# Where modulation rows, a feed-forward split and a rounding stand in a three-layer kernel

## Chip, cores and metric

One core of one Trainium2 chip runs the whole program in one launch. The metric is the device time of one execution in microseconds (us). TensorE is called PE, VectorE DVE, ScalarE ACT, GpSimd POOL; SyncE (SP) only issues transfers. DMA is the set of 16 engines that move data between device memory and on-chip memory.

## The reference, cut to what matters

The input is 256 tokens of 1024 float32 features. Three layers follow one another:

```python
h = x                                        # first_block, two layers
h = h + rg_lru_block(rms_norm(h, mix_norm[0]))            # layer 0
h = h + swiglu_ffn(rms_norm(h, ffn_norm[0]))
h = h + stick_breaking_attention(rms_norm(h, mix_norm[1]))  # layer 1
h = h + swiglu_ffn(rms_norm(h, ffn_norm[1]))
x = rms_norm(h, final_norm)
...
mod = silu(c) @ w_ada + b_ada                # second_block: 6 * 1024 modulation values
sh1, sc1, g1, sh2, sc2, g2 = split(mod, 6)
x = x + g1 * (mixed_attentions(rmsnorm(x) * (1 + sc1) + sh1) @ w_out)
x = x + g2 * moe(rmsnorm(x) * (1 + sc2) + sh2)            # 32 experts, top 2 of one group
return rmsnorm(x, final_g)
```

In `rg_lru_block` the input product has a recurrent branch (convolution, two sigmoid gates from products with `gate_w`, a scan) and a gate branch (a gelu); their product goes through `w_out`. `swiglu_ffn` has 2816 hidden columns. `c` is a single row of 1024, so `mod` is a product of one row with a 1024 x 6144 matrix (25 MB) that nothing needs before the third layer.

## The kernel before

The program is written by hand, one instruction list per engine, with semaphores. Activations lie feature-major: 8 tiles of 128 features by 256 tokens. Weights come in units of 2 MB into a ring of three places (`RING`), or, for the feed-forwards, in steps of 256 hidden columns into two slots. SP issues all of these loads in one order and waits for the place to be free.

**Products in parts.** Most float32 products are made as three matmuls of a coarser type. A weight is split first: ACT rounds it into a high part (`hi_unit`, `split_g`, `split_u` on ACT), DVE subtracts to get the low part (`lo_unit`, `split_g`, `split_u` and `subtract` on DVE, line 1057), and PE multiplies high by high, low by high, high by low (lines 1645, 1670, 1735). So PE follows DVE, which follows ACT, which follows a load.

**A feed-forward** has 11 steps. In each PE makes gate and up products (`gate_up`, line 1735, 96 matmuls) and the down product of the step before (`down`, line 1670, 48 matmuls). DVE does in each step: `split_g` of the next step, the product of silu and up, its two parts, `split_u` of the next step, the split of the down weight, and in layer 0 then some units of the modulation.

**Modulation rows.** The 48 columns of `mod` are 24 units of two. POOL loads a unit (1 MB, line 599) into one of two places in the ring when the unit two before is used up; DVE multiplies each of its two columns with the row silu(c) and sums (`ada_product`, line 1135). `ADA_FROM` says which units step n of the first feed-forward does at its end: 2, 2, 3, 2, 3, 2, 3, 2, 2, 1 units in steps 0 to 9, unit 22 at the end of step 10 and unit 23 in its middle. The ring place is free for `k0` (a weight of the attention) when all 24 are used. The row silu(c) is made on ACT (line 807) just before the norm of the first feed-forward; `silu_c` tells DVE.

**A norm** goes ACT squares (line 655), PE sums over features (line 1615), ACT root (lines 659, 660), DVE scales (line 1032). It cannot start until DVE has added the residual (line 1189 after the LRU, line 1198 after the feed-forward). DVE and PE have little to do meanwhile: a pause.

**The gates** of the LRU: after convolution of half the features (line 1103 ends it) PE makes four gate tiles, then four more for the other half (line 1691). The tiles go round four banks, so the fifth waits until ACT has taken the first with its sigmoid (line 728). In ACT's list the rounding of `gb0` (first half of the gate branch weight) stands ahead of all sigmoids and that of `gb1` behind the fourth.

**The experts.** After routing, each of 32 experts needs 6 MB. SP loads three ahead into three slots and issues the next expert's weights when PE has used a slot. Before the first of these (expert 3) SP issues two small transfers, `gate_tile` (line 566): the row g2 spread over 128 partitions, which DVE needs ahead of its work for expert 0 (lines 1550 to 1558).

**At the start** PE runs 24 small matmuls on ones (line 1677), then the sums of the first norm, then the product with `rec0` (line 1636).

## Time and profile before

| what | value |
|---|---|
| median of 3 runs | 1341.46 us (1340.09 to 1345.76) |
| the profiled execution | 1343.59 us |
| its span, first to last instruction | 1341.8 us |
| mean granted clock of PE | 0.943 of full |
| PE matmul busy | 1154.9 us (86%) |
| DVE busy | 634.5 us (47%) |
| ACT busy | 412.1 us (31%) |
| DMA, mean over the span | 270 GB/s |
| modulation rows | DVE line 1135, 56.1 us busy in 48 products |

PE is busy through the first two thirds of the span, where it moves little data; from about 905 us on DMA is busy in every slice at about 429 GB/s and PE waits for expert weights. A microsecond saved ahead of that stage moves the whole stage.

### The profile page before, as it was taken

To read this page: it belongs to the slowest core of one execution; us is meant where nothing else is said; L and a number is where in the kernel's file an instruction comes from. 1 tells how busy PE (TensorE), PEld (TensorE's weight loads), DVE (VectorE), ACT (ScalarE), POOL (GpSimd) and SP (SyncE) were. 2 spreads that over 40 slices of the span, in tenths; PEclk is the share of its full clock that TensorE was granted. 3 is DMA by queue.
4 is the path that set the end of the run, shared out by engine and by line. 5 is a ranking of instruction groups with operands and counts; after the bars stand their busy time and mean duration, and the time that the engine had idled before them with its cause. 6 is when DMAs were issued, how large, how long until landed. Compare 5 with 4: busy or idle time off the path is not lost.

```text
span 1341.8 us, 22971 instructions
## 1 busy us (share of the span) xinstructions
PE 1154.9 (86%) x9327; PEld 933.6 (70%) x9329; DVE 634.5 (47%) x997; ACT 412.1 (31%) x519; POOL 31.6 (2%) x69
## 2 busy tenths in 40 slices
PE   9998999999989899999899999967876568567666
PEld 8898999998977899999799888842332223223223
DVE  5686777765435254455634887471211112111213
ACT  3854333333357243334514565250000000000001
POOL 0000000000000000000000000000000000000000
PEclk9999999999999999999899999978988889888889
DMA  9565988872550575552644433499999999999996
GB/s 350 205 256 179 334 288 326 287 268 91 186 188 1 203 260 177 178 177 72 121 139 170 144 127 134 179 370 422 429 429 427 430 428 428 429 427 429 429 427 262
DMA packets 99464, 362.47 MB, mean 270 GB/s; under 512 B 4160, under 2 KB 51664, under 8 KB 84176
## 3 DMA queue, kind: packets, MB, share of 16 engines
q1 hardware_dynamic: 95376, 335.32, 65.5%
q0 software_dynamic: 3888, 26.24, 4.9%
q8 instruction: 43, 0.70, 0.2%
q14 instruction: 13, 0.11, 0.0%
q10 hardware_dynamic: 144, 0.10, 0.0%
HBM read 360.58 MB, written 1.06 MB: 270 GB/s over the span
## 4 chain that ended last, share of the span: by engine, by line
PE 64%; DMA 24%; DVE 5%; ACT 4%; issue 2%; SPq 0%; POOLq 0%; POOL 0%; DVEq 0%; ACTq 0%
DMA wbuf<-in_w_up 21%; PE ps L1735 17%; PE ps L1670 13%; PE ps L1645 8%; PE ps L2030 6%; PE ps L1908 4%; PE ps L1636 3%; PE ps L1654 3%; DMA wbuf<-in_w_ada 2%; PE ps L1615 2%; DVE parts L1057 2%; PE ps L2050 1%; PE ps L2080 1%; DVE wbuf L1135 1%; DMA wbuf<-in_lru_w_in 1%
## 5 line engine op out<-in xcount | busy, mean ns | idle before, releaser
L1735 PE MATMUL ps<-big_parts,parts 128*128 128x256 f32 x2112 | 266.4, 289 | 12.2 <-DVE parts L1057 6.7
L1735 PEld LDWEIGHTS ps<-big_parts,parts 128*128 128x128 f32 x2112 | 262.7, 197 | 14.9 <-DVE parts L1057 7.3
L1057 DVE TENSOR_TENSOR parts<-wbuf,parts 128x2048 fp32r<-128x2048 f32 x88 | 200.0, 2290 | 132.0 <-ACT parts L797 43.4
L2030 PE MATMUL ps<-wbuf,big 128*32 128x256 f32 x2176 | 166.7, 472 | 108.7 <-DMA wbuf<-in_w_up 97.8
L2030 PEld LDWEIGHTS ps<-wbuf,big 128*32 128x32 f32 x2176 | 86.1, 134 | 203.0 <-issue 101.4
L1670 PE MATMUL ps<-big_parts,parts 128*128 128x256 f32 x1344 | 166.1, 283 | 1.1 <-DVE parts_f L1259 1.1
L1670 PEld LDWEIGHTS ps<-big_parts,parts 128*128 128x128 f32 x1344 | 163.3, 192 | 1.3 <-issue 1.3
L989 ACT ACTIVATE big<-ps 128x128 f32<-128x128 f32 x33 | 9.1, 277 | 417.3 <-PE ps L2030 417.3
L1562 DVE TENSOR_TENSOR big<-big,ps 128x128 f32<-128x128 f32 x33 | 9.5, 289 | 265.1 <-ACT big L989 265.1
L1645 PE MATMUL ps<-parts_f,parts 128*128 128x256 f32 x672 | 97.3, 284 | 0.0
L1645 PEld LDWEIGHTS ps<-parts_f,parts 128*128 128x128 f32 x672 | 87.9, 192 | 0.2
L2080 PE MATMUL ps<-wbuf,big 128*32 128x512 f32 x544 | 65.4, 596 | 16.2 <-DVE big L1550 16.2
L1057 DVE TENSOR_TENSOR parts<-wbuf,parts_f 128x2048 fp32r<-128x2048 f32 x28 | 63.3, 2289 | 23.5 <-ACT parts_f L688 23.5
L2050 PE MATMUL ps<-big 64*128 64x512 f32 x272 | 68.3, 615 | 3.6 <-DVE big L1558 2.6
L707 ACT ACTIVATE parts<-wbuf 128x2048 fp32r<-128x2048 f32 x22 | 42.1, 1915 | 87.5 <-PE ps L1735 80.7
L1135 DVE SCALAR_TENSOR_TENSOR wbuf<-wbuf,big 128x1024 f32<-128x1024 f32 x48 | 56.1, 1221 | 20.0 <-DMA wbuf<-in_w_ada 20.0
L797 ACT ACTIVATE parts<-wbuf 128x2048 fp32r<-128x2048 f32 x20 | 38.3, 1913 | 60.6 <-PE ps L1670 60.6
L688 ACT ACTIVATE parts_f<-wbuf 128x2048 fp32r<-128x2048 f32 x28 | 52.4, 1904 | 3.3 <-PE ps L1645 3.3
L1908 PE MATMUL ps<-parts_f 128*128 128x256 f32 x256 | 48.5, 291 | 1.0 <-DVE parts L1057 1.0
L2050 PEld LDWEIGHTS ps<-big 64*128 64x128 f32 x272 | 23.6, 186 | 35.6 <-issue 33.9
L688 ACT ACTIVATE parts<-wbuf 128x2048 fp32r<-128x2048 f32 x22 | 40.9, 1908 | 23.4 <-DMA wbuf<-in_lru_w_in 22.8
L1636 PE MATMUL ps<-big,wbuf 128*128 128x256 f32 x192 | 43.9, 391 | 3.8 <-ACT big L665 2.2
(312 smaller groups left out, 1332.4 us busy)
## 6 DMA issues: line engine op xcount, KB each, us to landing
wbuf<-in_w_down SPq DMA_DIRECT2D x32, 2048.0 KB, 37.9
wbuf<-in_w_gate SPq DMA_DIRECT2D x31, 2048.0 KB, 32.6
wbuf<-in_w_up SPq DMA_DIRECT2D x31, 2048.0 KB, 37.1
wbuf<-in_ffn_w_in SPq DMA_DIRECT2D x44, 1024.0 KB, 11.4
wbuf<-in_w_ada POOLq DMA_DIRECT2D x24, 1024.0 KB, 8.3
wbuf<-in_ffn_w_out SPq DMA_DIRECT2D x22, 1024.0 KB, 5.0
wbuf<-in_w_in SPq DMA_DIRECT2D x10, 2048.0 KB, 8.0
wbuf<-in_attn_w_qkv SPq DMA_DIRECT2D x6, 2048.0 KB, 7.9
```

The source lines that it names most:

```text
L688: nc.scalar.activation(halves(unit_parts(name)[0])[i], halves(unit_view(name))[i], ACT.Copy).then_inc(w_hi, 1)
L707: nc.scalar.activation(fg_part[0], ffn_views(slot)[0], ACT.Copy).then_inc(fg_hi, 1)
L1057: nc.vector.tensor_tensor(lo, whole, hi.bitcast(F32), ALU.subtract).then_inc(done, 1)
L1135: ins = nc.vector.scalar_tensor_tensor(out=w, in0=w, scalar=1.0, in1=c_row, op0=ALU.mult, op1=ALU.mult, accum_out=ada[:, at:at + 1])
L1636: ins = mm(b[:, d * 256:(d + 1) * 256], w[:, k, (m + d) * P:(m + d + 1) * P], rhs[:, k], start=(k == 0), stop=(k == kn - 1))
L1645: ins = mm(b[:, d * 256:(d + 1) * 256], w[pw][:, k, (m + d) * P:(m + d + 1) * P], rhs[px][:, k], start=(k == 0 and i == 0), stop=(k == kn ...
L1670: ins = mm(ps[:, 4 + f // 2, (f % 2) * 256:(f % 2 + 1) * 256], w[:, k, f * P:(f + 1) * P], r, start=(first and k == 0 and f % 2 == 0), sto ...
L1735: ins = mm(ps[:, b, d * 256:(d + 1) * 256], w[pw][:, k, d * P:(d + 1) * P], h_part_of[px][:, k], start=(k == 0 and i == 0), stop=(k == KC ...
L1908: ins = mm(ps[:, c % 2, d * 256:(d + 1) * 256], w[pw][:, k, m * P:(m + 1) * P], x_part[px][:, k], start=(k == 0 and i == 0), stop=(k == KC ...
L2030: ins = mm(at, rows, gu_place[s][:, :, k, r * P:(r + 1) * P], start=(k == 0), stop=(k == KC - 1))
L2050: ins = mm(ps[:, 4 + 2 * c + h, :], comb[q][rows, c * P:(c + 1) * P], yE[q][rows, :], start=False, stop=stop, skip_group_check=True)
L2080: ins = mm(ps[r * WIN:(r + 1) * WIN, 2, :], hidT[:, f * WIN:(f + 1) * WIN], d_place[s][:, f, h * 512:(h + 1) * 512], start=(i == 0), stop= ...
```

## The change

The modulation units are laid out anew: unit 0 is done before the residual that follows the LRU, step n of the first feed-forward does units 2n + 1 and 2n + 2, step 10 does unit 21 in its middle and unit 22 at its end, and unit 23 comes after that feed-forward's residual. For unit 0, ACT makes silu(c) earlier, between its `split_g` and `split_u`. DVE's `split_u` of the first step moves behind the residual. ACT rounds `gb0` after the two sigmoids of gate tile 0 and `gb1` after those of tile 1. The warm-up has 20 matmuls in place of 24. The two transfers of `gate_tile` go from SP's list to POOL's; SP waits for the first gate and up product (`first_gu`) in their place.

```diff
-WARM_UP = 24
+WARM_UP = 20
-ADA_FROM = (0, 2, 4, 7, 9, 12, 14, 17, 19, 21, 22)
+ADA_FROM = tuple(range(1, ADA_UNITS - 1, 2))
@@ SP
-            sp.wait_ge(mod_stored, 48)
-            sp.wait_ge(spread_pe, 2)
-            for h in range(2):
-                sp.dma_start(gate_tile[h * HALF_ROWS:(h + 1) * HALF_ROWS], mod_dram[2:3, h * 512:(h + 1) * 512].to_broadcast([HALF_ROWS, 512])).then_inc(gate_in, 16)
+            sp.wait_ge(first_gu, 1)
@@ POOL, after the slot numbers and before its wait for info_ready
+            pool.wait_ge(mod_stored, 48)
+            pool.wait_ge(spread_pe, 2)
+            for h in range(2):
+                pool.dma_start(gate_tile[h * HALF_ROWS:(h + 1) * HALF_ROWS], mod_dram[2:3, h * 512:(h + 1) * 512].to_broadcast([HALF_ROWS, 512])).then_inc(gate_in, 16)
@@ ACT
             hi_unit("rec1")
-            hi_unit("gb0")
             for n in range(4):
...
-                if n == 1:
-                    hi_unit("gb1")
+                if n < 2:
+                    hi_unit(f"gb{n}")
...
             split_g(0, ffn_loads(0, 0))
+            act.wait_ge(c_in, 16)
+            nc.scalar.activation(c_row, c_row, ACT.Silu).then_inc(silu_c, 1)
             wait_used(act, "lo0")
             split_u(0)
...
-            act.wait_ge(c_in, 16)
-            nc.scalar.activation(c_row, c_row, ACT.Silu).then_inc(silu_c, 1)
@@ DVE
             split_g(0, 0)
-            split_u(0, 0)
...
             dve.wait_ge(silu_c, 1)
+            ada_unit(0)
             wait_used(dve, "lo1")
             for k in range(KC):
...
+            split_u(0, 0)
@@ DVE, a step of the feed-forward
-                            ada_unit(ADA_UNITS - 1)
+                            ada_unit(ADA_UNITS - 3)
...
-                        for u in range(ADA_FROM[n], ADA_FROM[n + 1] if following else ADA_UNITS - 1):
+                        for u in range(ADA_FROM[n], ADA_FROM[n + 1]) if following else (ADA_UNITS - 2,):
                             ada_unit(u)
@@ DVE
             add_residual(f"ffn0_{FFN_STEPS - 1}")
+            ada_unit(ADA_UNITS - 1)
```

## Rows read from the trace of the kernel before

**Rows 1.** The page's chain of work that ended last: shares of the span by engine.

```profile
PE 64%; DMA 24%; DVE 5%; ACT 4%; issue 2%; SPq 0%; POOLq 0%; POOL 0%; DVEq 0%; ACTq 0%
```

**Rows 2.** Timeline, an undisturbed step: start, duration, engine, line, operation, [idle <- releaser].

```profile
283.61 5.92 PE L1670 MATMUL ps<-big_parts,parts 128*128 128x256 f32 x48
...
289.37 11.68 PE L1735 MATMUL ps<-big_parts,parts 128*128 128x256 f32 x96
```

**Rows 3.** Timeline, the first stall in the first feed-forward.

```profile
163.48 0.53 POOL L599 DMA_DIRECT2D wbuf<-in_w_ada  x1 [14.46 <-DVE wbuf L1135]
...
172.01 1.23 DVE L1135 SCALAR_TENSOR_TENSOR wbuf<-wbuf,big 128x1024 f32<-128x1024 f32 x1 [6.54 <-DMA wbuf<-in_w_ada]
...
176.65 13.26 PE L1735 MATMUL ps<-big_parts,parts 128*128 128x256 f32 x96 [2.76 <-DVE parts L1057]
```

**Rows 4.** Busy time by stretch: length, PE, PEld, DVE, ACT, POOL, clock, DMA share, GB/s.

```profile
133.40:156.50 23.10, 23.10 (x195) 23.10 (x194) 19.43 (x21) 8.64 (x6) 1.59 (x3) 1.00 1.01 374
156.50:272.10 115.60, 108.89 (x866) 108.28 (x866) 85.19 (x96) 37.38 (x24) 7.93 (x15) 0.96 0.83 300
```

**Rows 5.** Line 1135 alone: durations (min/median/max ns), first to last start, what it waited for.

```profile
L1135 DVE SCALAR_TENSOR_TENSOR wbuf<-wbuf,big x48: 1217/1222/1227, 128.9 to 306.7; 128x1024 f32<-128x1024 f32 x48
...
  DMA wbuf<-in_w_ada: 20.0, 4
```

**Rows 6.** Timeline, end of the LRU and norm of the first feed-forward.

```profile
75.65 23.09 PE L1670 MATMUL ps<-big_parts,parts 128*128 128x256 f32 x192
...
98.17 1.06 ACT L807 ACTIVATE big<-big 128x1024 f32<-128x1024 f32 x1
...
99.37 3.22 DVE L1189 SCALAR_TENSOR_TENSOR xT<-ps,cols,xT 128x256 f32<-128x256 f32 x8
...
101.22 3.72 PE L1615 MATMUL ps<-big,cst 128*128 128x256 f32 x16 [2.48 <-ACT big L655]
...
105.93 0.88 DVE L1032 SCALAR_TENSOR_TENSOR big<-xT,cols,rstd 128x256 f32<-128x256 f32 x2 [3.34 <-ACT rstd L660]
```

**Rows 7.** Timeline, the gate tiles of the LRU.

```profile
39.46 5.09 DVE L1103 SCALAR_TENSOR_TENSOR big<-big,cols 128x256 f32<-128x256 f32 x12
39.62 3.71 ACT L688 ACTIVATE parts<-wbuf 128x2048 fp32r<-128x2048 f32 x2 [18.87 <-DMA wbuf<-in_lru_w_in]
...
44.65 0.84 ACT L728 ACTIVATE wbuf<-ps,cols 128x256 f32<-128x256 f32 x2
...
45.63 7.14 PE L1691 MATMUL ps<-big,wbuf 128*128 128x256 f32 x32 [1.51 <-ACT wbuf L728]
```

**Rows 8.** Timeline, last step of the first feed-forward and the norm behind it.

```profile
301.51 1.23 DVE L1135 SCALAR_TENSOR_TENSOR wbuf<-wbuf,big 128x1024 f32<-128x1024 f32 x1 [1.94 <-DMA wbuf<-in_w_ada]
...
308.00 37.33 SPq L493 DMA_DIRECT2D wbuf<-in_attn_w_qkv  x3
312.61 2.48 DVE L1198 TENSOR_TENSOR xT<-ps,xT 128x512 f32<-128x512 f32 x4 [4.64 <-PE ps L1670]
...
318.73 3.25 DVE L1032 SCALAR_TENSOR_TENSOR big<-xT,cols,rstd 128x256 f32<-128x256 f32 x8 [3.64 <-ACT rstd L660]
```

**Rows 9.** Timeline, PE's first product with a loaded weight.

```profile
11.62 14.08 PE L1636 MATMUL ps<-big,wbuf 128*128 128x256 f32 x64
```

**Rows 10.** Line 566 alone, the gate rows: starts, and issue to landing.

```profile
L566 SPq DMA_DIRECT2D big<-mod_dram x2: 518/555/592, 894.6 to 895.2; - x2
...
DMA to landing us min/median/max: 3.0/3.7/4.5
```

**Rows 11.** Who reads the routing table: DVE's load of it, with its durations.

```profile
L1570 DVEq TENSOR_LOAD <-info x1: 554/554/554, 899.8 to 899.8; - x1
```

**Rows 12.** Timeline, expert 0 on DVE, and SP's load for expert 5.

```profile
900.90 0.29 DVE L1550 COPY big<-ps 128x128 f32<-128x128 f32 x1 [2.85 <-PE ps L2073]
...
926.59 0.33 SPq L469 DMA_DIRECT2D wbuf<-in_w_gate  x1
```

**Rows 13.** Line 610 alone, the slot numbers from POOL's queue: issue (first start 870.1) to landing.

```profile
DMA to landing us min/median/max: 8.2/8.2/8.2
```

## The prediction, made before the changed kernel ran

> **What bounds the kernel now.** I read the chain of work that ended last first: most of it is PE, a quarter DMA [rows 1]. In order of time the DMA share is the wait for expert weights in the last third. So the span has two parts: up to the start of the expert loads PE's own order sets the time, with short gaps where it waits for DVE or ACT; after that the loads set it, and their length is fixed by 32 experts of 6 MB. Whatever is saved in the first part moves the second part as a block, if the expert loads start earlier by as much. The next view is the timeline of each place that the diff touches, and the last one the busy time by stretch, to see whether PE or DMA had room there.
>
> The places differ in kind. In the first feed-forward a step with two units costs PE 5.76 us for down (283.61 to 289.37) and 11.52 us for gate and up, 17.28 us in all, without a gap [rows 2]. In a step with three units the third must be loaded into a place that was just given up: POOL issues at 163.48, DVE gets it at 172.01, 8.5 us later, after 6.54 us idle, and PE starts its next product 2.76 us late and needs 13.26 us for it [rows 3]. Where nothing precedes it, the same 96 matmuls take 11.68 us [rows 2]: the rest is the lower clock after the gap (mean granted clock 0.96 in this stretch against 1.00 in the one before it, where PE never paused [rows 4]).
>
> **The even spread.** The loads of the units cost 20.0 us of DVE's waiting in four waits [rows 5]. Three of them are the third units of steps 2, 4 and 6, all inside 156.5 to 272.1. There PE goes through six steps. Without stalls six steps are 6 x 17.28 = 103.7 us; they took 115.6 us [rows 4]. The difference, **11.9 us**, is what the three third units cost. Of it 6.7 us is PE idle (115.60 less 108.89 busy) and the rest is clock.
>
> Is anything else late once they are gone? DVE: the stretch holds 15 units; one unit is two products and two reads, 2 x 1.22 us and a little [rows 5], and twelve units in place of fifteen leave DVE below its 85.19 busy us, in 103.7 [rows 4]. DMA: a step moves three feed-forward pieces and two units of 1.05 MB, 5.24 MB in 17.28 us, 303 GB/s; the stretch before moved 374 GB/s without stopping PE [rows 4]. The new unit order keeps two places: unit 1 is there beforehand, units 3 and 4 are asked for at the end of step 0 as units 2 and 3 were, and each has a whole step to land where 8.5 us are needed [rows 3]. So I take all of 11.9. The bounds are 11.0 to 12.0: below if one step still meets a late piece.
>
> **The pause after the LRU.** PE's last sum of the LRU ends at 75.65 + 23.09 = 98.74. DVE starts the residual only at 99.37, for two reasons: its `split_u` (2.29 us, as every subtraction of line 1057 on the page) had started late, since ACT's half waits until 32 of PE's 192 sums are left, at 94.9, and takes 1.9 us; and silu(c) ends at 98.17 + 1.06 = 99.23 [rows 6]. Behind silu(c) ACT must load a table, 1.28 us, to about 100.5, before it squares; PE starts the sums at 101.22, after 2.48 us for ACT [rows 6]. With the change silu(c) and its table lie in ACT's wait for PE before 94.9; `split_u` follows to 96.9 and the table load to 98.2. The residual can start at 98.8, its first pair is done 0.85 us later, ACT squares in 0.63 us, and the sums start near 100.35: **0.9 us** earlier. Unit 0 takes 2.4 us of DVE; DVE is through with the splits before it by about 94.8, so it ends at 97.2, 1.5 us before PE. Its weights are asked for when `gb1` is used up, at 75.8. Behind the residual (3.22 us, to 102.0) `split_u` runs to 104.3, and the root comes only 0.9 us before 105.93 [rows 6], at about 105.0: hidden with 0.7 us to spare. The SP load that waits for this `split_u` (step 2) goes 5 us later and is needed 20 us later. Bounds: 0 if DVE is late with unit 0, 1.2 if the row that ends last is even earlier.
>
> **The gate tiles.** ACT rounds `gb0` from 39.62, when its load lands, for 3.71 us, then loads the sigmoid's table, and takes the first tile at 44.65; PE's second four tiles start at 45.63 after 1.51 us for ACT [rows 7]. With the sigmoids of tile 0 first, ACT is no longer last: the convolution is, which DVE ends at 39.46 + 5.09 = 44.55. PE starts at about 44.65: **1.0 us** earlier. The rounding of `gb0` ends about 45.2 instead of 43.3, but its two subtractions on DVE stand behind that same convolution and take 4.5 us to 49.1; PE comes to them at 44.65 + 7.14 = 51.8. `gb1` then is rounded before the sigmoids of tile 2, which must free the bank for PE at 51.8: tile 0 done at 41.5, `gb0` at 45.2, two pairs of sigmoids at 46.8, `gb1` at 50.6, the next pair, 0.84 us [rows 7], at about 51.5: tight. Bounds: 0 to 1.1.
>
> **The end of the feed-forward.** In step 10 DVE already waits 1.94 us for a unit until 301.51 [rows 8]; the same place and the same release serve unit 21, with one more unit in flight behind it. 0 to 0.5 us later is hidden: its parts of hidden values were ready about 1 us before PE's down product. Unit 23 runs after the residual (312.61 + 2.48 = 315.1) for 2.4 us to 317.5 and the root comes at 318.73 [rows 8]: hidden with 1.2 us to spare. What waits for it is the load of `k0` on SP, at 308.00 now [rows 8], then at 317.5; 2 MB land some 8 us later (the page's issues), at 325.5, and ACT turns to it after `q0`, at 333.9. Nothing behind it on SP could go earlier. Cost 0.
>
> **The warm-up.** Eight instructions less on PE, some 0.7 us. But PE's product with `rec0` starts at 11.62 when its load lands, after a short idle time [rows 9]. Gain 0, bounds 0 to 0.4; the gap grows to about 1.1 us, less than the 1.51 us [rows 7] after which the tiles still ran at full pace.
>
> **The gate rows.** SP issues them at 894.6 and 895.2; they land 3.0 and 4.5 us later, at 899.7 at the latest [rows 10]. DVE's next act is the load of the routing table at 899.8 [rows 11], so it was waiting for them. At 900.90 it takes expert 0's hidden values, released by PE [rows 12]. About 1.1 us lie between, so the slack is near 0. Behind this copy stand expert 0's down product, the loop of experts and at its first turns SP's next loads, such as the one at 926.59 [rows 12], where the queue is nearly empty. A delay D here moves the end by D. SP gains 1 us for expert 3's load, which is worth nothing since the load at 926.59 waits for PE. POOL has room: its other work comes at 900.5. When will the rows land from POOL's queue? The nearest row is the slot numbers, 256 KB as these are, from the same queue beside expert loads: 8.2 us [rows 13]; from the second issue at 895.2 that is 903.4, D = 3.6. But these are two halves, the first starts before expert 3's load, and only the second has to take turns: half of the excess over a quiet landing, which puts it near 900. The lower bound is an earlier landing, D = 0, as PE then decides. I take **D = 0.3**, bounds 0 to 3.6.
>
> The Trainium skill ("SBUF — State Buffer", "SBUF: two separate sides") speaks against this move: descriptors of a transfer from POOL's queue are written by GpSimd, and VectorE in some float32 operations locks it out of their shared port. By it the rows would start only when DVE pauses. No run here shows it yet; what it would give is the third rival.
>
> **Sum.** 11.9 + 0.9 + 1.0 - 0.3 = 13.5 us. The profiled execution took 1343.59 us with a span of 1341.8, so it should become 1330.1 with a span of 1328.3. The median of the runs is 2.1 us below the profiled execution; from 1341.46 it should become **1328.0 us**.
>
> **The rivals.**
> 1. *The gate rows land late by turns.* With the slot numbers' 8.2 us, D = 3.6: 1341.46 - 13.8 + 3.6 = 1331.3. For it: the same queue, the same size, expert loads beside it. Against it: one load there, five before. Chance 0.15.
> 2. *Only the spread pays.* The small pauses turn out to be filled (the bank at 51.5, unit 0, the root): 1341.46 - 11.9 + 0.3 = 1329.9. For it: margins of 0.3 to 0.7 us. Chance 0.12.
> 3. *POOL's descriptors wait for DVE.* Should they wait for a pause of DVE, the first one begins at 900.90 - 2.85 = 898.05 [rows 12]; with 3.0 to 4.5 us [rows 10] from there the rows land at 901.0 to 902.5, D = 1.3 to 2.8, middle 2: 1329.7. Chance 0.12.
> 4. *The third wait only changes place.* If a unit took longer than a step leaves it, the even spread would wait in every step and the 11.9 us would stay: 1341.46 - 1.6 = 1339.9. Against it: 8.5 us to land in a step of 17.28. Chance 0.03.
> 5. *Slower than before: DMA becomes the bound of the first feed-forward.* Eleven steps of 5.24 MB with no slack are slower than before if each takes over 17.28 + 13.5 / 11 = 18.5 us, so if DMA gave less than 283 GB/s with these pieces. At 280 a step takes 18.7 us and the end is 1328.0 + 11 x 1.42 = 1343.6. For it: 300 GB/s at a share of 0.83; against it: that same share, and 374 GB/s in the stretch before [rows 4]. Chance 0.02.
>
> **How the numbers follow.** The forecast has a chance of 0.56, 1326.5 to 1329.3. The range also takes in rivals 1 to 3 and, at the low end, the case that everything small pays fully and the first turns of the expert loop, where PE stands for some us with no wait in the trace, go better by 2 us: 1325.3 to 1332.0 leaves out about 0.15. Measurement of this kernel cannot tell less than about 0.5% (6.7 us) from no change. Over that faster: the forecast and rivals 1 to 3, 0.56 + 0.15 + 0.12 + 0.12 = 0.95. Within it: rival 4, 0.03. Slower: rival 5, 0.02.
>
> **What would show it.** In the changed trace: DVE waits for the modulation loads once, not four times; steps 2 to 7 take 17.28 us each with 11.68 us products and a clock of 1.00; the sums of the first feed-forward's norm start about 1.6 us behind PE's last sum in place of 2.5; PE's second gate tiles follow the convolution; the root of the third norm still comes after unit 23. The prediction is wrong if DVE's load of the routing table comes later, against the end of PE's gather, than now (late gate rows), if DVE or ACT waits for feed-forward weights in each step, or if the time between DVE's copy for expert 0 and the load for expert 5, now 25.7 us, has changed by more than 2 us.

## The result and the profile after

| what | before | after |
|---|---|---|
| median of 4 runs | 1341.42 us (1340.09 to 1345.76) | 1326.66 us (1324.31 to 1330.84) |
| the profiled execution | 1343.59 us | 1327.39 us |
| its span | 1341.8 us | 1325.6 us |
| mean granted clock of PE | 0.943 | 0.947 |

The ratio is 0.9897, with a 95% interval of 0.9864 to 0.9931. The forecast was 1328.0 us, with a range of 1325.3 to 1332.0. The total is as forecast, in part by luck: one term of the sum, the cost of the late gate rows, was 3.7 us too small, and 6.1 us that were in no term made up for it.

The page of after, its busy times and the chain that ended last, shares of the span by engine (before: [rows 1]):

```profile
PE 1143.6 (86%) x9319; PEld 922.7 (70%) x9321; DVE 634.0 (48%) x997; ACT 412.5 (31%) x519; POOL 32.7 (2%) x71
...
PE 68%; DMA 22%; DVE 5%; ACT 3%; issue 2%; SPq 0%; DVEq 0%; POOL 0%; POOLq 0%; ACTq 0%
```

The kinds of bound are the same. PE's share of the chain rose and DMA's fell, as it should when waits for modulation units go away.

**The first feed-forward.** After, the busy time by stretch (length, PE, PEld, DVE, ACT, POOL, clock, DMA share, GB/s). These are the six steps of [rows 4], which now begin at 153.94, and a view of line 1135 with what it waited for (before: [rows 5]):

```profile
153.94:257.60 103.66, 103.66 (x866) 103.66 (x866) 78.63 (x84) 37.40 (x24) 6.37 (x12) 1.00 0.85 304
```

```profile
L1135 DVE SCALAR_TENSOR_TENSOR wbuf<-wbuf,big x48: 1215/1219/1224, 93.4 to 301.6; 128x1024 f32<-128x1024 f32 x48
...
  DMA wbuf<-in_w_ada: 0.9, 1
```

PE is busy for the whole 103.66 us at full granted clock, where the same six steps took 115.60 with PE busy for 108.89 and a clock of 0.96 [rows 4]. DVE waits once for a unit, 0.9 us, in place of 20.0 us in four waits [rows 5].

**The small places.** Timeline of after: the gate tiles (before: [rows 7]), then the end of the LRU and the norm behind it (before: [rows 6]). Columns: start, duration, engine, line, operation, [idle <- releaser].

```profile
39.21 5.09 DVE L1103 SCALAR_TENSOR_TENSOR big<-big,cols 128x256 f32<-128x256 f32 x12
...
44.35 7.17 PE L1693 MATMUL ps<-big,wbuf 128*128 128x256 f32 x32 [0.48 <-DVE big L1103]
...
46.65 3.72 ACT L689 ACTIVATE parts<-wbuf 128x2048 fp32r<-128x2048 f32 x2 [0.29 <-DMA wbuf<-in_lru_w_in]
```

```profile
93.36 1.22 DVE L1135 SCALAR_TENSOR_TENSOR wbuf<-wbuf,big 128x1024 f32<-128x1024 f32 x1
...
97.52 3.23 DVE L1189 SCALAR_TENSOR_TENSOR xT<-ps,cols,xT 128x256 f32<-128x256 f32 x8 [1.80 <-PE ps L1672]
...
99.11 3.72 PE L1617 MATMUL ps<-big,cst 128*128 128x256 f32 x16 [1.63 <-ACT big L656]
...
100.67 2.28 DVE L1057 TENSOR_TENSOR parts<-wbuf,parts 128x2048 fp32r<-128x2048 f32 x1
...
103.83 0.88 DVE L1032 SCALAR_TENSOR_TENSOR big<-xT,cols,rstd 128x256 f32<-128x256 f32 x2 [0.88 <-ACT rstd L661]
```

The second gate tiles follow the convolution (releaser L1103 on DVE; before it was ACT's sigmoid), and PE's gap is 0.48 us in place of 1.51. After the LRU the residual now waits for PE, not for `split_u` or silu(c), and the sums start 1.63 us behind PE's last sum, before 2.48. The subtraction at 100.67 is the `split_u` that was moved; it is over 0.9 us before the scale at 103.83.

**The gate rows.** Line 611 of after, which issues them from POOL, with their landing (before: [rows 10]); DVE's load of the routing table (before: [rows 11]); and the timeline of POOL, SP, DVE and PE there (before: [rows 12]):

```profile
L611 POOL DMA_DIRECT2D big<-mod_dram x2: 528/530/533, 874.9 to 875.4; - x2
...
DMA to landing us min/median/max: 3.7/6.4/9.1
```

```profile
L1572 DVEq TENSOR_LOAD <-info x1: 550/550/550, 884.5 to 884.5; - x1
```

```profile
875.33 0.34 SPq L469 DMA_DIRECT2D wbuf<-in_w_gate  x1
...
885.65 0.29 DVE L1552 COPY big<-ps 128x128 f32<-128x128 f32 x1 [7.79 <-issue]
...
886.09 3.64 PE L2082 MATMUL ps<-wbuf,big 128*32 128x512 f32 x16 [5.44 <-DVE big L1552]
```

The first half lands 3.7 us after its issue, at 878.5. The second, issued at 875.4, lands 9.1 us later, at 884.4, and at 884.5 DVE loads the routing table. That is 5.3 us behind the end of PE's gather (875.20 + 4.01); before it was 0.4 us (895.38 + 4.01 = 899.39, load at 899.77). From there on DVE is last where PE was: before, the copy of expert 0's hidden values was released by PE [rows 12], now PE stands 5.44 us for DVE, and its down product behind that gap takes 3.64 us, at a granted clock of 0.50, where it takes 1.92 us at 1.00 when the gap is short (that row is shown with the first experiment).

**Where 16.2 us of span went**, by the starts of the same instructions in the two traces:

| stretch | before | after | gain |
|---|---|---|---|
| start to the first product with `rec0` | 11.62 | 11.38 | 0.24 |
| to the second gate tiles | 34.01 | 32.97 | 1.04 |
| to the LRU's sums | 30.02 | 30.04 | 0.0 |
| to the sums of the first feed-forward's norm | 25.57 | 24.72 | 0.85 |
| to its first down product | 32.19 | 31.74 | 0.45 |
| to its residual | 179.20 | 167.24 | 11.96 |
| to the attention's scores | 78.03 | 78.03 | 0.0 |
| to the product behind the scores | 36.33 | 34.71 | 1.62 |
| to the residual of the second feed-forward | 223.68 | 224.22 | -0.54 |
| to the residual of the third layer's attentions | 215.89 | 211.32 | 4.57 |
| to the spread product | 26.03 | 25.97 | 0.06 |
| to the end | 449.2 | 453.3 | -4.0 |

The sum of the terms that the change explains is 0.24 + 1.04 + 0.85 + 11.96 - 4.0 = 10.1 us. The rest, 0.45 + 1.62 + 4.57 - 0.54 = 6.1 us, lies in stretches that hold no term of the forecast.

### The profile page after: what moved, and what is told of

It reads as the page before. It is cut to its first block, busy times and chain, and to the rows that moved or that the text cites. A ratio compares the mean times of both kernels' runs of the same rounds, so it can differ in the third digit from the quotient of the medians.

```text
span 1325.6 us, 22956 instructions
## 1 busy us (share of the span) xinstructions
PE 1143.6 (86%) x9319; PEld 922.7 (70%) x9321; DVE 634.0 (48%) x997; ACT 412.5 (31%) x519; POOL 32.7 (2%) x71
## 4 chain that ended last, share of the span: by engine, by line
PE 68%; DMA 22%; DVE 5%; ACT 3%; issue 2%; SPq 0%; DVEq 0%; POOL 0%; POOLq 0%; ACTq 0%
DMA wbuf<-in_w_up 21%; PE ps L1737 19%; PE ps L1672 15%; PE ps L1647 9%; PE ps L2032 7%; PE ps L1638 3%; PE ps L1656 3%; PE ps L1910 3%; PE ps L2082 2%; PE ps L1617 2%; PE ps L2052 1%; DVE parts L1057 1%; PE ps L1806 1%; DMA wbuf<-in_lru_w_in 1%; ACT parts_f L689 1%
## 5 line engine op out<-in xcount | busy, mean ns | idle before, releaser
L1737 PE MATMUL ps<-big_parts,parts 128*128 128x256 f32 x2112 | 261.6, 285 | 5.6 <-DVE big_parts L1057 5.1
L1737 PEld LDWEIGHTS ps<-big_parts,parts 128*128 128x128 f32 x2112 | 258.2, 194 | 7.7 <-issue 5.8
L2032 PEld LDWEIGHTS ps<-wbuf,big 128*32 128x32 f32 x2176 | 86.2, 135 | 202.7 <-issue 94.0
L1672 PE MATMUL ps<-big_parts,parts 128*128 128x256 f32 x1344 | 166.1, 283 | 1.1 <-DVE parts_f L1261 1.1
L1672 PEld LDWEIGHTS ps<-big_parts,parts 128*128 128x128 f32 x1344 | 163.3, 192 | 1.3 <-issue 1.3
L708 ACT ACTIVATE parts<-wbuf 128x2048 fp32r<-128x2048 f32 x22 | 42.1, 1914 | 75.5 <-PE ps L1737 68.8
L799 ACT ACTIVATE parts<-wbuf 128x2048 fp32r<-128x2048 f32 x20 | 38.3, 1913 | 60.5 <-PE ps L1672 60.5
L2082 PEld LDWEIGHTS ps<-wbuf,big 128*32 128x32 f32 x544 | 17.1, 110 | 46.0 <-issue 45.3
```

Source lines behind the costliest of these rows:

```text
L708: nc.scalar.activation(fg_part[0], ffn_views(slot)[0], ACT.Copy).then_inc(fg_hi, 1)
L1672: ins = mm(ps[:, 4 + f // 2, (f % 2) * 256:(f % 2 + 1) * 256], w[:, k, f * P:(f + 1) * P], r, start=(first and k == 0 and f % 2 == 0), sto ...
L1737: ins = mm(ps[:, b, d * 256:(d + 1) * 256], w[pw][:, k, d * P:(d + 1) * P], h_part_of[px][:, k], start=(k == 0 and i == 0), stop=(k == KC ...
L2032: ins = mm(at, rows, gu_place[s][:, :, k, r * P:(r + 1) * P], start=(k == 0), stop=(k == KC - 1))
L2082: ins = mm(ps[r * WIN:(r + 1) * WIN, 2, :], hidT[:, f * WIN:(f + 1) * WIN], d_place[s][:, f, h * 512:(h + 1) * 512], start=(i == 0), stop= ...
```

## The experiments

The theory after the result: the spread pays all that it was forecast to, the two small pauses as well, and the gate rows cost 4 us because their second half is issued behind the load of expert 3 and has to share the DMA engines with it ("turns" in what follows). The rivals: the rows are late because POOL's queue is slow as such or its descriptors wait for DVE; or the 4 us at the end are no effect of the rows at all.

In the first group each part of the change was undone or done alone. **The changed kernel with the gate rows back on SP:**

```diff
 # SP, ahead of the load of expert 3
+            sp.wait_ge(mod_stored, 48)
+            sp.wait_ge(spread_pe, 2)
+            for h in range(2):
+                sp.dma_start(gate_tile[...], mod_dram[2:3, ...]...).then_inc(gate_in, 16)
-            sp.wait_ge(first_gu, 1)
 # and the same lines gone from POOL
```

> The changed kernel with one part undone: SP issues the two gate-row transfers again, as before the change. Theory A (late rows): in the changed kernel's trace DVE's load of the routing table comes 12.2 us after PE's spread product starts, before the change 7.2 us; this 5 us is on the path, so without it the kernel takes 1326.7 - 4.5 = about 1322 us and DVE's copy for expert 0 comes again about 8.3 us behind the spread product. Theory B (hidden): the expert loads set the end whatever DVE does for expert 0, so the time stays at 1326.7 within 1 us.

Measured: 1327.61 us, ratio to before 0.9884 (0.9856 to 0.9911), span 1325.5. Line 566 of this kernel, the timeline at its first expert:

```profile
DMA to landing us min/median/max: 2.8/3.5/4.2
```

```profile
886.56 0.29 DVE L1551 COPY big<-ps 128x128 f32<-128x128 f32 x1 [2.98 <-PE ps L2074]
...
887.00 1.92 PE L2081 MATMUL ps<-wbuf,big 128*32 128x512 f32 x16 [0.47 <-DVE big L1551]
```

From the same queue as before the rows land as before, PE is last again, and from the spread product to the copy it takes 8.47 us, with POOL 13.31. To the end it takes 447.4 us in place of 453.3. Yet the span is the same, since this execution was 4.4 us slower between the residuals of the second feed-forward and the third layer (215.73 against 211.32), where the two kernels are alike. The total of about 1322 us that theory A asked for did not come in the other executions either: the median of six is 1327.61. So A is borne out in the trace and not in the time.

**The kernel before with only the gate rows moved to POOL** (the diff above, the other way):

> The kernel before with one part of the change alone: the gate-row transfers on POOL's queue, SP waiting for the first gate and up product. Theory A (late rows): 1341.4 + 4.5 = about 1346 us, the rows landing about 9 us after their issue instead of 3.0 to 4.5. Theory B (hidden): 1341.4 within 1 us.

Measured: 1343.61 us (12 runs), ratio 1.0015 (0.9992 to 1.0038), span 1344.3. The rows land 4.9 and 8.3 us after their issue; spread product to copy 12.59 us, to the end 452.8. So the move alone costs 3.6 us in the trace (449.2 before), and -1 to +5 us by the interval of the ratio: the total is too coarse for it, and lies between the two theories.

**The kernel before with only the modulation units, silu(c) and `split_u` moved** (`ADA_FROM`, unit 0, unit 21 and 22, unit 23 as in the change; warm-up, gate rows and the rounding as before):

```diff
-ADA_FROM = (0, 2, 4, 7, 9, 12, 14, 17, 19, 21, 22)
+ADA_FROM = tuple(range(1, ADA_UNITS - 1, 2))
... # and on ACT and DVE the places of silu(c), split_u and units 0, 21, 22, 23 as in the change
```

> The kernel before with the new places of the modulation units alone: even spread, unit 0 and the earlier silu(c) in the pause after the LRU, the first split_u behind the residual, unit 23 in the next norm's pause. From the prediction's terms 11.9 + 0.9: 1341.4 - 12.8 = 1328.6 us. In the pair of traces the way to PE's first expert product shrank by 20.2 us where the terms give 14; if the rest belongs to the spread (theory C: fewer stalls also mean a better clock later), 1322 to 1325; if it is chance of the clock in one execution (theory D), 1328 to 1330.

Measured: 1326.59 us, ratio 0.9879 (0.9855 to 0.9904), span 1327.9. Its busy time over the six steps and the wait of its line 1135:

```profile
153.94:257.60 103.66, 103.66 (x867) 103.66 (x865) 78.60 (x85) 37.39 (x24) 6.35 (x12) 1.00 0.85 303
```

```profile
  DMA wbuf<-in_w_ada: 1.0, 1
```

From the first down product to the residual it takes 167.24 us, and the pause after the LRU has its 0.85 us (24.72 us to the sums); the gate tiles stay at 34.08. This part alone gives all that can be measured of the change. Its execution has both long values of the two stretches without an edit (36.34 and 215.89 us), so the spread does not bring the short ones with it, which speaks against theory C.

**The kernel before with only the rounding moved:**

```diff
-            hi_unit("gb0")
             for n in range(4):
...
-                if n == 1:
-                    hi_unit("gb1")
+                if n < 2:
+                    hi_unit(f"gb{n}")
```

> The kernel before with the rounding of gb0 and gb1 between the gate tiles alone. By the prediction's term 1.0 us less: 1340.4 us, PE's second four gate tiles starting about 0.1 us behind the end of the convolution on DVE. If the gate branch then waits for its rounded weights, no gain: 1341.4.

Measured: 1341.31 us (12 runs), ratio 0.9998 (0.9976 to 1.0020). In the trace the second gate tiles come 32.88 us after the `rec0` product, before 34.01: the 1.1 us are there, and the total can't show them. But that product started 0.4 us later here (12.03 against 11.62), and the load of `gb0`, which held ACT up before [rows 7], does not follow it: it lands at 39.4 to 39.6 in both, and in the kernel with only the gate rows moved. From the start of the span the tiles come at 44.90 against 45.63, 0.7 us earlier; in the kernel with only the gate rows moved, where the product started at 12.88, the stretch is 32.88 us without this edit. So the 1.0 us is the worth of the rounding only where `rec0` starts early. Its first feed-forward brought a surprise. It has the three third units, yet the stretch to the residual takes 175.55 us, not 179.20. The three products behind the stalls, in this kernel:

```profile
177.15 11.77 PE L1734 MATMUL ps<-big_parts,parts 128*128 128x256 f32 x96 [2.74 <-DVE parts L1056]
...
214.75 11.78 PE L1734 MATMUL ps<-big_parts,parts 128*128 128x256 f32 x96 [2.79 <-DVE parts L1056]
...
251.58 11.78 PE L1734 MATMUL ps<-big_parts,parts 128*128 128x256 f32 x96 [2.02 <-DVE parts L1056]
```

and in the kernel before, the second and third of them (the first is in [rows 3]):

```profile
214.91 13.27 PE L1735 MATMUL ps<-big_parts,parts 128*128 128x256 f32 x96 [1.96 <-DVE parts L1057]
...
253.21 13.29 PE L1735 MATMUL ps<-big_parts,parts 128*128 128x256 f32 x96 [1.99 <-DVE parts L1057]
```

The idle times are alike, 7.55 and 6.71 us in all. Behind them the product takes 0.1 us more than the undisturbed 11.68 in one execution and 1.6 us more in the other. The busy time of the first of these products, here and in the kernel before, ends in the mean granted clock, the DMA share and GB/s:

```profile
177.15:188.92 11.77, 11.77 (x98) 11.77 (x99) 11.70 (x14) 1.92 (x1) 1.06 (x2) 1.00 0.57 201
```

```profile
176.65:189.90 13.25, 13.25 (x98) 13.25 (x99) 12.86 (x14) 1.92 (x1) 1.06 (x2) 0.87 0.63 226
```

So three third units cost 175.54 - 167.24 = 8.3 us or 11.96 us, by whether the clock falls behind the gap; in the kernel with only the gate rows moved, where it fell once, it was 9.8.

**A second group: where the rows are issued from, and when.** The changed kernel was run again beside them: 1329.35 us (7 runs), ratio 0.9923 (0.9889 to 0.9958), span 1327.6.

> The changed kernel once more, on the chip and beside the runs of the next three. In two traces with the gate rows on POOL's queue the way from PE's spread product to the end takes 452.8 and 453.3 us, in four with them on SP's queue 447.4 to 449.5 us: 4.4 us more. In times this has not come out: 1326.7 against 1327.6 us (with the rows back on SP). Theory A (late rows on the path): this takes 4.4 us more than the kernel with early rows. Theory B (chance of the traces): the same within 1 us. Again 452 to 454 us from spread product to end are expected by A, 447 to 450 by B.

Its trace repeats the first one: 167.24 us to the residual, rows landing 3.5 and 8.7 us after their issue, 13.01 us to the copy, 455.3 us to the end, and the same short values in the stretches without an edit (34.71 and 211.28 us).

**SP waits with expert 3 until the gate rows are there:**

```diff
 # SP
             sp.wait_ge(first_gu, 1)
+            sp.wait_ge(gate_in, 32)
             sp.wait_ge(info_ready, 1)
```

> The changed kernel with the gate rows on POOL's queue, but SP's load for expert 3 waits until they have landed, so no expert load is under way beside them. Theory T (turns): they land in 3 to 4.5 us, DVE's copy comes 8.4 to 9 us behind the spread product, and SP's load for expert 3 some 2 to 3 us later than in the changed kernel. Theory G: they land after 9 us all the same, the copy comes at 12 to 13 us, SP's load some 7 us later, and the time is 4 to 7 us more than the changed kernel's.

Measured: 1329.09 us, ratio 0.9925 (0.9898 to 0.9953). Line 612, POOL's issue of the rows, and the timeline beside it:

```profile
L612 POOL DMA_DIRECT2D big<-mod_dram x2: 533/537/541, 879.3 to 879.8; - x2
...
DMA to landing us min/median/max: 2.7/2.9/3.1
```

```profile
879.22 0.22 DVE L1543 TENSOR_SCALAR big<-small,cst 128x32 f32<-128x32 f32 x1
...
879.37 0.22 DVE L1544 TENSOR_SCALAR big<-small,cst 128x32 f32<-128x32 f32 x1
...
883.32 0.34 SPq L469 DMA_DIRECT2D wbuf<-in_w_gate  x1
```

Same queue, same size, and DVE as busy with the same instructions as in the changed kernel (there this loop runs over POOL's issue at 874.87 too). Only the load of expert 3 is missing beside them, and the second half lands in 3.1 us, not 9.1. That speaks against the rival in which POOL's descriptors wait for DVE, and so does the changed kernel itself: there DVE is idle from 877.9 on, for the 7.79 us ahead of its copy at 885.65, and the second half still does not land until 884.4. The price is paid elsewhere. SP's load of expert 3 comes 6.6 us behind the spread product in place of 3.0, and to the end it takes 451.9 us, 1.4 us less than in the changed kernel. By the Trainium skill ("SBUF — State Buffer", "SBUF: two separate sides") VectorE can lock GpSimd out of the port over which it writes descriptors; no run here shows such a delay with DVE's instructions of this place.

**The rows from ACT's queue,** issued between ACT's two copies of the spread rows:

```diff
 # ACT
+            act.wait_ge(mod_stored, 48)
+            for h in range(2):
+                act.dma_start(gate_tile[...], mod_dram[2:3, ...]...).then_inc(gate_in, 16)
             nc.scalar.activation(weight_bc, ps[:, 2, :], ACT.Copy).then_inc(spread_ev, 1)
```

> The changed kernel with the gate rows issued from ACT's queue, which writes its descriptors in hardware as SP's does, but has rings of its own. Theory T (turns): what makes the rows late is that each DMA engine takes turns between the ring of the expert weights and the other ring, so they land some 9 us after issue here too, DVE's copy for expert 0 comes 12 to 13 us behind the spread product, and the time is the changed kernel's. Theory G (GpSimd's descriptors, held up by DVE): they land after 3.0 to 4.5 us as from SP, the copy comes about 8.4 us behind the spread product, and the time is 4 us less.

Measured: 1325.74 us, ratio 0.9915 (0.9884 to 0.9946), span 1321.6. Issue and landing, and the first load of expert 3:

```profile
L981 ACTq DMA_DIRECT2D big<-mod_dram x2: 507/559/611, 874.2 to 874.8; - x2
...
DMA to landing us min/median/max: 2.8/3.4/4.1
```

```profile
875.41 0.34 SPq L469 DMA_DIRECT2D wbuf<-in_w_gate  x1
```

Both halves are issued before the load of expert 3, and both are quick. The 9 us that the expectation gave for turns did not come, since it took for granted that the load would be ahead. This left open whether ACT's queue is better or the 0.6 us by which it was earlier.

**The same from ACT, but behind both copies:**

```diff
             nc.scalar.activation(weight_bc, ps[:, 2, :], ACT.Copy).then_inc(spread_ev, 1)
+            act.wait_ge(mod_stored, 48)
+            act.wait_ge(spread_ev, 2)
+            for h in range(2):
+                act.dma_start(gate_tile[...], mod_dram[2:3, ...]...).then_inc(gate_in, 16)
```

> The changed kernel with the gate rows issued from ACT's queue behind both of ACT's copies of the spread rows, so about 876.2 and 876.8, 0.9 us behind SP's first load of expert 3 (875.3); in the run before, ACT issued them 1.2 us ahead of that load and they landed within 4.1 us. If what counts is the load of expert 3 being in the queues first (turns), the rows land 6 to 9 us after their issue, DVE's load of the routing table comes at 883 to 886 and from the spread product to expert 5's load 35 to 37.5 us pass. If what counts is POOL's queue, ACT's rows land again within 3 to 4.5 us, the table is loaded at 880 to 881.5 and the interval is 31.5 to 33 us. The total can't tell the two apart: 1325 to 1330 us either way.

Measured: 1329.39 us, ratio 0.9935 (0.9911 to 0.9959), span 1325.6. ACT reached the issue earlier than expected, so that its first half still went ahead of the load and only the second behind it:

```profile
L983 ACTq DMA_DIRECT2D big<-mod_dram x2: 507/560/613, 875.4 to 875.9; - x2
...
DMA to landing us min/median/max: 3.4/6.3/9.1
```

```profile
875.78 0.34 SPq L469 DMA_DIRECT2D wbuf<-in_w_gate  x1
```

3.4 and 9.1 us: ACT's queue gives the same two landings as POOL's (3.7 and 9.1), and DVE's load of the routing table comes at 885.1, as expected for the case that the load of expert 3 decides. What decides is whether that load is in the queues when a half is issued, not whose queue carries it; a tenth of a microsecond behind it is enough.

**Where the 5 us go** can be read from the DMA packets in the kept traces. Here are the queues of the changed kernel from the last packet of the first half to the first of the second, and from there to the landing (packets, MB, share of the 16 engines; q1 is SP's queue with the expert load, q0 POOL's):

```profile
q1 hardware_dynamic: 55, 0.90, 91.9%
```

```profile
q1 hardware_dynamic: 101, 1.39, 92.5%
q0 software_dynamic: 48, 0.13, 9.6%
...
```

For 2.4 us (878.02 to 880.38) only the load's packets move. In the six traces in which the second half is issued behind the load, its first packet moves 4.5 to 5.0 us after the issue (4.6 from ACT's queue); where it is issued ahead of it, or the load is held back, 1.4 to 1.9 us. From the first packet to the landing it takes 3.7 to 4.5 us in place of 1.8 to 2.7. So of the 5 us about 3 lie ahead of the first packet, and only some 2 in the mixing of the two transfers, packets of 16 KB at 0.6 us each with packets of 2 or 4 KB. The Trainium skill ("DMA: Bandwidth & Descriptors", "Queues, rings and completion order") says that a DMA engine serves its queues in turn, a packet from each. The second part agrees with that; the 3 us ahead of the first packet are longer than one such turn, and why they come no run here shows.

**The rows long before** (issued by POOL at 815.6, into a place that is free earlier, with the spread rows at another place):

```diff
-        spread = flat(10752, 1024).rearrange("p (j t) -> p j t", j=2)
+        spread = [flat(0, 512), flat(1024, 512)]
 # POOL, ahead of its wait for x_ready
+            pool.wait_ge(route_sum, 1)
+            for h in range(2):
+                pool.dma_start(gate_tile[...], mod_dram[2:3, ...]...).then_inc(gate_in, 16)
 # DVE, ahead of clearing yE[0] and comb[0]
+            dve.wait_ge(spread_pe, 2)
```

> The changed kernel with the gate rows loaded early: the two spread tiles lie at the start of the working area, so the place of the gate rows is free some 60 us sooner, and POOL asks for them behind the router weights. Nobody waits for them any more. Theory A (late rows): DVE's copy for expert 0 about 8.3 us behind the spread product, 448 to 449 us from there to the end, and 4.4 us less than the changed kernel: 1322.3 if that is 1326.7. Theory B: no difference.

Measured: 1328.04 us, ratio 0.9909 (0.9879 to 0.9939). The rows land in 6.4 and 7.2 us and nobody waits for them: spread product to copy 8.22 us, to the end 448.6. They are slow here too, and here too a load of 2 MB had been issued before them, SP's for `w_out` at 813.3. The trace is as theory A has it; the total of 1322.3 us is not.

**Does the end follow the rows?** From the spread product to the end, over all traces: where the second half is issued behind the load of expert 3 (changed kernel twice, rows moved alone, ACT behind both copies, and the two kernels below) 453.3, 455.3, 452.8, 452.9, 452.2 and 453.4 us. Where it isn't: 449.2 (before), 449.5, 448.7, 447.4, 448.6 and 449.4, and 451.9 where SP holds expert 3 back for it. The means of the first two groups, 453.3 and 448.8, are 4.5 us apart and the groups do not overlap. So for the traces the rival that it has nothing to do with the rows falls. In the timed runs the same 4.5 us can't be told: ratios 0.9897 to 0.9935 with late rows, 0.9879 to 0.9925 without, each with an interval of 0.002 to 0.004 to either side. The means of the runs point the same way and not as far: 1344.0 us (12 runs) with only the rows moved against 1341.5 (23) before, and 1329.0 (7) in the changed kernel's second group against 1326.7 (12) with the rows early or ahead on ACT, so 2.5 and 2.3 us more, with an uncertainty of 2.6 and 3.6.

**The third group: the changed kernel with one third unit in a step,**

```diff
-ADA_FROM = tuple(range(1, ADA_UNITS - 1, 2))
+ADA_FROM = (1, 3, 5, 8, 9, 11, 13, 15, 17, 19, 21)
```

> The changed kernel with unit 7 moved from step 3 of the first feed-forward to step 2: one third unit in a step, the rest even. If a third unit is what costs, the stretch from the first down product to the residual of the first feed-forward grows from 167.2 us by a third of what three third units cost (8.3 to 12.0 us in the kernels that had them): 2.8 to 4.0 us, to 170.0 to 171.2, with one idle time of DVE of about 6 us for the load of unit 7. If the stalls in the kernel before came from the whole stretch being short of DMA, one third unit is absorbed and it stays at 167.2 to 167.6.

Measured: 1332.71 us, ratio 0.9942 (0.9926 to 0.9958). The stretch to the residual is 172.95 us, 5.7 more than with the even spread. The timeline of DVE and PE at the stall:

```profile
169.60 1.22 DVE L1135 SCALAR_TENSOR_TENSOR wbuf<-wbuf,big 128x1024 f32<-128x1024 f32 x1 [6.54 <-DMA wbuf<-in_w_ada]
...
174.24 14.48 PE L1737 MATMUL ps<-big_parts,parts 128*128 128x256 f32 x96 [2.76 <-DVE parts L1057]
```

and the busy time of that product's stretch (columns as above):

```profile
174.24:188.55 14.31, 14.31 (x96) 14.31 (x97) 10.65 (x10) 1.91 (x1) 0.53 (x1) 0.78 0.65 241
```

The idle times of DVE and PE, 6.54 and 2.76 us, are those of [rows 3] to the hundredth, and the third unit is confirmed as their cause. The product takes 2.80 us more than 11.68, at a mean granted clock of 0.78, more than any of the three in the kernel before. So the stretch grew by more than the 2.8 to 4.0 us that were expected.

**The changed kernel with 24 warm-up matmuls:**

```diff
-WARM_UP = 20
+WARM_UP = 24
```

> The changed kernel with the warm-up back at 24 small matmuls. As forecast (PE waits for the load of rec0 anyway) the product with rec0 starts at the same time, 11.4 to 11.6 us, with a shorter idle time ahead of it, and every later interval is unchanged: 0 us. If the gap ahead of this product costs clock, the 24 are better by up to 0.4 us between rec0 and the second gate tiles (32.97 us now).

Measured: 1328.71 us, ratio 0.9912 (0.9890 to 0.9934). PE's first product with `rec0` starts at 12.13, with no idle time before it, and with 20 at 11.38 after 0.66 us:

```profile
12.13 1.24 PE L1638 MATMUL ps<-big,wbuf 128*128 128x256 f32 x5
```

```profile
11.38 1.99 PE L1638 MATMUL ps<-big,wbuf 128*128 128x256 f32 x8 [0.66 <-DMA wbuf<-in_lru_w_in]
```

Over all traces the start is 11.54 to 12.88 with 24 (five of them, median 12.03) and 11.31 to 11.98 with 20 (eight, median 11.58). So with 24 PE's own work can be last, against the expectation, and eight fewer instructions were worth 0.2 us in the profiled pair and 0.45 us by these medians, not nothing. Every later interval up to the product behind the scores is unchanged within 0.3 us.

## Why the prediction was right, and where it wasn't

- **The even spread: right.** 11.9 us forecast, 11.96 measured, with PE without a gap and a clock of 1.00. What the text lacked is that 11.9 belongs to this one execution: the idle part is steady (6.7 to 7.6 us for three), the clock part is not (0.3 to 4.8 us in the three products). That the pair came out at 11.96 is thus partly luck. The bounds of 11.0 to 12.0 were too narrow below; 8.3 would have been the end.
- **What would be late next: right.** DVE waits 0.9 us once, for unit 21 at 286.99, the one place where the prediction saw 0 to 0.5 us of more delay, and PE doesn't feel it.
- **The pause after the LRU: right,** 0.85 for 0.9 us. Unit 0 runs from 93.36 (forecast 94.8); the moved `split_u` ends 0.9 us before it would matter (forecast 0.7).
- **The gate tiles: right,** 1.04 for 1.0 us, released by the convolution as forecast (0.7 us from the start of the span where the rounding alone was moved). The tight place, `gb1` between the sigmoids, held: the stretch behind it is 30.04 us, before 30.02.
- **The end of the feed-forward: right.** Unit 23 ends at 302.85, 1.3 us before the root ends at 304.18 (forecast 1.2), and `k0` is asked for at 302.88; to the scores it takes 78.03 us in both kernels.
- **The warm-up: a misread row.** [Rows 9] shows no idle time before 11.62, and its sums end at that moment. The text said that PE waits for the load. It didn't, so the gain was 0.24 us where 0 was taken, within the bounds.
- **The gate rows: the term that was mis-sized.** D was forecast 0.3 with an upper end of 3.6; the profiled pair shows 4.0 us at the end (4.5 as the mean of groups). The first step was right: the slack is near 0, and D reaches the end. The second was right in kind: the first half goes ahead of expert 3, the second shares with it. What failed is the price: "half of the excess over a quiet landing" had no row behind it. The nearest row, the slot numbers' 8.2 us [rows 13], applied in full to the second half gives the order of what was measured (8.3 to 9.1 us in the five traces with POOL's queue), and the upper bound wanted a little more than that one row. Rival 1 was what happened in kind and in price (3.6 us). Of its mechanism, turns, the packets show some 2 of the 5 us of late landing; its total, 1331.3, was missed all the same, for the reason in the next point. One of the signs that the prediction had named as showing it wrong did come: DVE's load of the routing table stands 5.3 us behind the end of PE's gather, before 0.4 us. The other did not: from DVE's copy to the load for expert 5 it is 24.0 us (885.65 to 909.65), before 25.7.
- **What closed the gap: 6.1 us that no term held.** They lie mostly in two stretches that take one of two values in traces of kernels alike there. The stretch to the product behind the scores is 34.71 us in eight traces and 36.29 to 36.34 in five; from the second feed-forward's residual to the third layer's it is 211.3 to 211.6 in five, 214.2 in one and 215.7 to 215.9 in seven. Both values occur with and without the change: the kernel with only the rounding moved has both short ones, and the one with the rows back on SP both long ones. These are traces of different kernels that are alike in these stretches; the one kernel that was traced twice, the changed one, had the short values both times. That executions of one kernel differ too is shown only by their totals: those of the changed kernel in its second group go from 1321.93 us at a mean granted clock of 0.950 to 1333.6 at 0.943. The longer of the two stretches, in the changed kernel and with the rows back on SP (columns as above):

```profile
635.05:846.37 211.32, 199.76 (x1438) 184.47 (x1438) 128.52 (x242) 96.62 (x162) 3.99 (x5) 0.99 0.49 152
```

```profile
636.46:852.19 215.73, 204.41 (x1438) 188.61 (x1438) 128.85 (x242) 96.58 (x162) 3.98 (x5) 0.97 0.46 149
```

PE's busy time differs by 4.65 us in the same 1438 matmuls and its idle time by 0.24 us, the other way: it is all clock. So it is in the shorter stretch, 30.95 us busy at 1.00 against 32.57 at 0.95, with 3.76 us idle in both. Two rows stand for it, the product behind the norm of the attentions, first in the kernel with the rows back on SP, then in the changed one:

```profile
651.73 15.66 PE L1637 MATMUL ps<-big,wbuf 128*128 128x256 f32 x64 [2.16 <-ACT big L665]
```

```profile
650.17 14.05 PE L1638 MATMUL ps<-big,wbuf 128*128 128x256 f32 x64 [2.17 <-ACT big L666]
```

The same idle time ahead of it, 1.6 us of difference in the same 64 matmuls. In the profiled execution of before the long values fell together, in that of after the short ones.

So by terms the change was worth 10.1 us in these traces, not 13.5, and the profiled execution came out at 1327.39 us because 6.1 us more fell its way, most of it clock. The median of 1326.66, 14.8 us below that of before, holds some of the same luck; how much, the untraced runs do not show. The second comparison of the changed kernel, 0.9923, is nearer to the terms: 0.0077 x 1341.46 = 10.3 us, with an interval of 5.6 to 14.9.

- **Left open:** why the first packet of the second half waits 3 us more beside the load of expert 3, and what makes the clock fall behind a gap in one trace and not in another. Among the kernels run, the one with the rows on ACT ahead of the load has the lowest median and all parts of the change, but 1325.74 and 1326.66 us can't be told apart.

## What to carry to other kernels

Where one consumer takes from a ring at an uneven pace, take the pace that the ring's landing time allows: the third unit cost 2.0 to 2.8 us of PE each time, and up to 2.8 more in the product behind it. A small transfer that somebody waits for must be issued ahead of the next large load, in the same queue or in another; moving it to an idle engine's queue is worth nothing if that engine gets to it a tenth of a microsecond behind the load. And a gain of a few us that is read from one trace should be split into idle time, which repeats, and slow clock, which may not.

## What the runs showed of the hardware that was not expected

- A transfer of 128 KB landed 2.7 to 4.9 us after its issue if it went ahead of the expert load of 2 MB, and 8.3 to 9.1 us after it if that load had been issued up to 0.3 us before, from POOL's queue and from ACT's alike. Two such transfers behind another load of 2 MB, issued 2.2 us before (packets of 4 KB, not 16), landed in 6.4 and 7.2 us.
- Some 3 of the 5 us passed before the first packet of the late transfer moved (4.5 to 5.0 us after its issue in place of 1.4 to 1.9).
- Behind a PE gap of 2 to 2.8 us the same 96 matmuls took 11.77, 13.26 or 14.48 us, at a mean granted clock of 1.00, 0.87 and 0.78, so the last two in part at the lower of the two levels (1.2 GHz). The gap had the same length, 2.74 to 2.76 us, in all three, in three different kernels.
